# Differential-attention probabilities transposed by VectorE squares and a DRAM round trip, head index innermost, values later in TensorE's order

## The reference

```python
# differential attention: two 64-dim maps per head, value dim 128
sc = jnp.einsum('bqhcd,bkhcd->bhcqk', qb, kf) * scale      # c = 0, 1
p = jax.nn.softmax(jnp.where(causal, sc, -jnp.inf), axis=-1)
attn = p[:, :, 0] - lam * p[:, :, 1]
oa = rms_norm(jnp.einsum('bhqk,bkhe->bqhe', attn, vf), subln_w) * (1 - lambda_init)
# sparse attention: an indexer scores keys, the 64 best causal keys per query are kept
score = jnp.einsum('bqhk,bqh->bqk', jax.nn.relu(jnp.einsum('bqhd,bkd->bqhk', qi, ki)), wi)
_, idx = lax.top_k(jnp.where(causal, score, -jnp.inf), 64)
ob = softmax(q . k_sel) @ v_sel
mix = concatenate([oa * silu(dg), ob * silu(sg)]);  x = x + rms_norm(mix @ w_out, post_w)
```

## Time and profile before

| | |
|---|---|
| median of three runs | 303.1 us (302.99 to 303.43) |
| the profiled execution, its own time | 302.85 us |
| its span, first to last instruction | 301.1 us |
| TensorE busy | 292.4 us (97%) |
| TensorE weight loads busy | 246.4 us (82%) |
| VectorE busy | 234.9 us (78%) |
| ScalarE busy | 163.9 us (54%) |
| GpSimd busy | 67.6 us (22%) |
| DMA queue of SyncE, share of 16 engines | 62.8% |
| granted TensorE clock, mean | 0.996 of full speed |

### The profile page before, as it was taken

The page is one execution under the profiler, slowest core; times in us unless marked ns, Lnnn a source line. Parts: engine busy times, 40 slices in busy tenths (PEclk is TensorE's granted clock), DMA queues, the critical chain, the costliest instruction groups (busy, mean ns, idle before and its releaser), DMA issues.

```text
span 301.1 us, 4401 instructions
## 1 busy us (share of the span) xinstructions
PE 292.4 (97%) x1568; PEld 246.4 (82%) x1568; DVE 234.9 (78%) x474; ACT 163.9 (54%) x284; POOL 67.6 (22%) x116
## 2 busy tenths in 40 slices
PE   8999999999999999999999999999999999999992
PEld 7799777788787888788888988778878788887892
DVE  4752989899999997955984786878999999787343
ACT  5986963736577473603665855473737747390101
POOL 6558210303030220101060740012303030210101
PEclk9999999999999999999999999999999999999998
DMA  7999959457518569860059799937653675742011
GB/s 242 370 371 386 371 214 354 135 143 227 195 69 210 209 211 303 191 201 23 0 158 369 242 350 250 325 108 204 209 150 131 146 272 152 202 70 72 0 70 70
DMA packets 62229, 60.01 MB, mean 199 GB/s; under 512 B 34560, under 2 KB 39424, under 8 KB 62208
## 3 DMA queue, kind: packets, MB, share of 16 engines
q1 hardware_dynamic: 61920, 59.47, 62.8%
q10 hardware_dynamic: 288, 0.26, 0.3%
HBM read 54.48 MB, written 5.24 MB: 198 GB/s over the span
## 4 chain that ended last, share of the span: by engine, by line
PE 40%; DVE 37%; ACT 8%; DMA 6%; POOL 4%; issue 3%; SPq 1%; POOLq 0%; DVEq 0%; ACTq 0%
DVE w_lo L987 14%; PE bank_a L470 8%; PE bank_a L461 7%; PE bank_a L466 7%; PE bank_s L618 6%; DMA w_raw<-in_w_in 6%; PE bank_a L618 5%; ACT xt_pbuf L831 4%; DVE work L1107 4%; DVE xt_pbuf L1124 3%; DVE top L1106 3%; DVE xt_pbuf L1140 3%; DVE mixn L1150 2%; DVE mixn L1036 2%; PE bank_s L559 1%
## 5 line engine op out<-in xcount | busy, mean ns | idle before, releaser
L987 DVE TENSOR_TENSOR w_lo<-w_raw,w_hi 128x2048 fp32r<-128x2048 f32 (+1 forms) x46 | 98.8, 2154 | 18.5 <-ACT w_hi L763 18.3
L763 ACT ACTIVATE w_hi<-w_raw 128x2048 fp32r<-128x2048 f32 (+1 forms) x46 | 81.9, 1784 | 31.9 <-PE bank_a L470 23.4
L461 PE MATMUL bank_a<-w_hi,h_hi 128*128 128x512 f32 (+1 forms) x272 | 72.5, 388 | 0.0
L470 PE MATMUL bank_a<-w_lo,h_hi 128*128 128x512 f32 (+1 forms) x272 | 70.0, 379 | 0.5 <-DVE w_lo L987 0.5
L466 PE MATMUL bank_a<-w_hi,h_lo 128*128 128x512 f32 (+1 forms) x272 | 69.9, 379 | 0.0
L470 PEld LDWEIGHTS bank_a<-w_lo,h_hi 128*128 128x128 f32 x272 | 49.7, 188 | 10.5 <-DVE w_lo L987 1.0
L466 PEld LDWEIGHTS bank_a<-w_hi,h_lo 128*128 128x128 f32 x272 | 49.8, 188 | 9.8
L461 PEld LDWEIGHTS bank_a<-w_hi,h_hi 128*128 128x128 f32 x272 | 47.9, 188 | 10.4 <-issue 2.7
L831 ACT ACTIVATE xt_pbuf<-xt_pbuf,st 128x128 f32<-128x128 f32 (+1 forms) x48 | 21.3, 444 | 25.1 <-DVE st L1124 25.1
L1417 POOL TENSOR_TENSOR rt<-nat,tab 128x256 f32<-128x256 f32 x10 | 7.4, 741 | 112.5 <-ACT nat L815 112.5
L815 ACT ACTIVATE nat<-bank_a,st 128x512 f32<-128x512 f32 x20 | 13.5, 681 | 19.6 <-PE bank_a L470 19.6
(11 more groups left out here) (196 smaller groups left out, 431.1 us busy)
## 6 DMA issues: line engine op xcount, KB each, us to landing
w_raw<-in_w_in SPq DMA_DIRECT2D x30, 1024.0 KB, 6.0
w_raw<-in_w_out SPq DMA_DIRECT2D x8, 1024.0 KB, 6.1
w_raw<-in_w_in SPq DMA_DIRECT2D x8, 584.0 KB, 7.3
turned<-mixn SPq DMA_DIRECT2D x20, 128.0 KB, 2.7
prm<-in_rows SPq DMA_DIRECT2D x2, 705.0 KB, 7.0
w_raw<-in_w_in SPq DMA_DIRECT2D x2, 512.0 KB, 6.3
xres<-in_x SPq DMA_DIRECT2D x2, 512.0 KB, 9.5
dqT<-turned SPq DMA_DIRECT2D x2, 512.0 KB, 5.9
```

The source lines that it names most:

```text
L461: pe.matmul(bank, h_hi[:, HALF * half + kk, tok], whi[:, kk, :], start=half == 0 and kk == 0, stop=False)
L470: mm = pe.matmul(bank, h_hi[:, HALF * half + kk, tok], wlo[:, kk, :], start=False, stop=half == 1 and kk == HALF - 1)
L763: act.activation(unit(w_hi, u), unit(raw, u), ACT.Copy).then_inc(hi_done.sem, 1)
L987: dve.tensor_tensor(unit(w_lo, u), unit(raw, u), unit(w_hi, u).bitcast(F32), ALU.subtract).then_inc(lo_done.sem, 1)
```

## The change

1. The three TensorE turns of the differential probabilities go (12 transposes a layer), and with them their three drains on VectorE. In their place stand three `dve.transpose` of 128x512, four `put` DMAs for each and one `get` for each. The squares are staged in `mixn`, and in the two halves of `nat[:, 1]`.
2. In all DRAM-turned tensors (queries of all three mixers, PD and PS) the slot (head, or block and head) becomes the innermost index. VectorE writes its squares with a step of 8 floats (4 floats for PD and PS0), the DRAM runs grow to 256 floats (128 for PD and PS0), and TensorE's stationary tile is read with that step (`gathered`).
3. In TensorE's order `values(0)` moves from behind `dsa_scores(12)` to behind `first(18)`, and `values(1)` from ahead of `second(18)` to behind `turn_mix(T_MD0)`. They wait for the landing of the DMAs in place of the drains.
4. The squares of the sparse queries are staged in `iqT` and not in `mixn`; so the drain of T_SK, which writes over `iqT`, waits for their `put`.
5. On VectorE one round of `choose(1, ...)` comes behind the combine of PD1B's heads, and `gate_dsa(0)` comes ahead of the drain of T_MD1. The T banks are numbered anew (13 uses a layer in place of 16).

```diff
-T_IK, T_DK, T_PD0, T_PD1A, T_SK, T_PD1B = 4, 5, 7, 8, 9, 11
-T_MD0, T_MD1, T_MS0, T_MS1 = 12, 13, 14, 15
+T_IK, T_DK, T_SK = 4, 5, 7
+T_MD0, T_MD1, T_MS0, T_MS1 = 9, 10, 11, 12
+IQS, DQS, SQS, PD0, PD1A, PD1B, PS0, PS1 = range(8)
...
+        def gathered(buf, s, parts=slice(0, P), slots=BLOCKS * HEADS):
+            return buf[parts, :].rearrange("p (t s) -> p s t", s=slots)[:, s, :]
+        def by_column(buf):
+            return buf.rearrange("p (j c s) -> p s j c", j=SQUARES, c=LANES)
...  SyncE
-                    to = scratch[n].rearrange("(j r) a (i c) -> i r a j c", j=SQUARES, i=SQUARES)[i]
+                    to = scratch[n].rearrange("(j r) i m -> i r j m", j=SQUARES)[i]
...
                     if u == 16:
                         sp.wait_ge(sq_squares.sem, sq_squares.at(layer, 1))
-                        put(2, squares, sq_put.sem)
+                        put(SQS, iqT, sq_put.sem)
+                        put_probs(layer, PD0)
                     if u == 17:
                         sp.wait_ge(sq_put.sem, sq_put.at(layer, 16 * SQUARES))
-                        get(2, sqT, sq_landed.sem)
+                        get(SQS, sqT, sq_landed.sem)
+                        put_probs(layer, PD1A)
+                        get_probs(layer, PD0)
+                    if u == 18:
+                        put_probs(layer, PD1B)
+                        get_probs(layer, PD1A)
+                        get_probs(layer, PD1B)
...  TensorE
-                        mm = pe.matmul(bank[:, i * n:(i + 1) * n], sqT[:, b, h, :],
+                        mm = pe.matmul(bank[:, i * n:(i + 1) * n], gathered(sqT, b * HEADS + h),
...
-                pe.wait_ge(combined.sem, combined.at(layer, 1))
-                turn_probs(T_PD0, 6, 0, HEADS)
                 diff_scores(10, 1, (2, 3))
                 second(15)
-                pe.wait_ge(combined.sem, combined.at(layer, 2))
-                turn_probs(T_PD1A, 8, 1, 2)
...
-                pe.wait_ge(combined.sem, combined.at(layer, 3))
-                turn_probs(T_PD1B, 10, 1, 2)
                 pe.wait_ge(t_drained.sem, t_drained.at(layer, T_SK + 2))
                 pe.wait_ge(sq_landed.sem, sq_landed.at(layer, sq_landed.per_layer))
                 dsa_scores(12, 0, range(HEADS))
-                pe.wait_ge(t_drained.sem, t_drained.at(layer, T_PD0 + 1))
-                values(0, 0, v_diff, [[slot(0, h)] for h in range(HEADS)], place(layer, DV, 0) + 1)
                 second(17)
                 first(18)
+                pe.wait_ge(prob_landed[PD0].sem, prob_landed[PD0].at(layer, 16))
+                values(0, 0, v_diff, [[gathered(pT[:, 0, :], h, slots=HEADS)] for h in range(HEADS)], ...)
                 dsa_scores(13, 1, (0, 1))
                 dsa_scores(14, 1, (2, 3))
-                pe.wait_ge(t_drained.sem, t_drained.at(layer, T_PD1B + 1))
-                values(1, 1, v_diff, ...)
                 second(18)
                 turn_mix(T_MD0, 0, 0)
+                pe.wait_ge(prob_landed[PD1A].sem, prob_landed[PD1A].at(layer, 16))
+                pe.wait_ge(prob_landed[PD1B].sem, prob_landed[PD1B].at(layer, 16))
+                values(1, 1, v_diff, ...)
                 first(19)
...  VectorE
-                    dve.transpose(squares, nat[:, slot, :, :].rearrange("p b n -> p (b n)")).then_inc(done, 1)
+                    dve.transpose(by_column(iqT[:, :] if rope == 4 else squares), nat[:, slot, :, :].rearrange("p b (f j c) -> p (b f) j c", j=SQUARES, c=LANES)).then_inc(done, 1)
...
+                turn_squares(1, 4, sq_squares.sem)
                 dve.wait_ge(dq_put.sem, dq_put.at(layer, 16 * SQUARES))
-                turn_squares(1, 4, sq_squares.sem)
+                turn_probs(PD0, 6)
                 split_lo(layer, 16)
                 combine(8, 1, 2, 0)
-                drain(T_PD0, pT[:, 0, :])
+                dve.wait_ge(sq_squares.sem, sq_squares.at(layer, 1))
+                turn_probs(PD1A, 8)
                 mask_scores(10, 1, 2, causal[:, :])
                 mask_scores(11, 1, 2, causal[:, :])
                 split_lo(layer, 17)
+                choose(1, 1)
+                combine(10, 1, 2, 2)
+                turn_probs(PD1B, 10)
                 choose(1, 2)
-                drain(T_PD1A, pT[:, 1, :])
-                combine(10, 1, 2, 2)
-                choose(1, 1)
                 mask_unchosen(1)
+                dve.wait_ge(sq_put.sem, sq_put.at(layer, 16 * SQUARES))
                 drain_pair(T_SK, skT)
                 split_lo(layer, 18)
-                drain(T_PD1B, pT[:, 2, :])
                 mask_scores(12, 0, 4, work[0][:, :])
...
+                gate_dsa(0)
                 drain_mix(T_MD1, m_hi, m_lo, 1, subln)
-                gate_dsa(0)
```

More of the change, by code:

```diff
@@ L86 @@
 ROW_N = sum(ROW.values())
-T_IK, T_DK, T_PD0, T_PD1A, T_SK, T_PD1B = 4, 5, 7, 8, 9, 11
-T_MD0, T_MD1, T_MS0, T_MS1 = 12, 13, 14, 15
-T_USES = 16
-PS0, PS1 = range(3, 5)
+T_IK, T_DK, T_SK = 4, 5, 7
+T_MD0, T_MD1, T_MS0, T_MS1 = 9, 10, 11, 12
+T_USES = 13
+IQS, DQS, SQS, PD0, PD1A, PD1B, PS0, PS1 = range(8)
+SLOT = {PD0: 0, PD1A: 1, PD1B: 2, PS0: 0}
 LANES = 32
@@ L175, in build_trunk @@
         squares = mixn[:, :, :].rearrange("p b n -> p (b n)")
-        prob_buf = {PS0: dkT[:, 0:2, :].rearrange("p f t -> p (f t)"), PS1: dqT[:, :, :, :].rearrange("p b f t -> p (b f t)")}
+        prob_buf = {PD0: mixn[:, 0, :], PD1A: nat[:, 1, 0, :], PD1B: nat[:, 1, 1, :], PS0: dkT[:, 0:2, :].rearrange("p f t -> p (f t)"), PS1: dqT[:, :]}
         A = [pb("bank_a0", [P, WIDTH]), pb("bank_a1", [P, WIDTH])]
@@ L240, in build_trunk @@
         rq_ready = count("rq_ready", BLOCKS)
-        prob_squares = count("prob_squares", 2)
-        prob_put = {n: count(f"prob_put{n}", 16 * SQUARES) for n in range(PS0, PS1 + 1)}
-        prob_landed = {n: count(f"prob_landed{n}", 16) for n in range(PS0, PS1 + 1)}
+        prob_squares = count("prob_squares", 5)
+        prob_put = {n: count(f"prob_put{n}", 16 * SQUARES) for n in range(PD0, PS1 + 1)}
+        prob_landed = {n: count(f"prob_landed{n}", 16) for n in range(PD0, PS1 + 1)}
         subln_ready = count("subln_ready", 1)
@@ L257, in build_trunk @@
         pool_setup = sem("pool_setup")
-        ends = (S[1], T[0])
+        ends = (S[1], T[1])
         last_ms = st[:, 153:154]
@@ L317, in put @@
                 for i in range(SQUARES):
[L318 to L319 removed]
+                    to = scratch[n].rearrange("(j r) i m -> i r j m", j=SQUARES)[i]
+                    sp.dma_start(to, buf[i * LANES:(i + 1) * LANES, :].rearrange("r (j m) -> r j m", j=SQUARES)).then_inc(written, 16)
             def put_probs(layer, n):
[L322 removed]
+                sp.wait_ge(prob_squares.sem, prob_squares.at(layer, n - PD0 + 1))
                 put(n, prob_buf[n], prob_put[n].sem)
@@ L640, in body @@
                     for n in range(2):
-                        for i in range(4):
-                            f, b = 2 * n + i // 2, i % 2
-                            mm = pe.transpose(S[n][:, i * P:(i + 1) * P], nat[:, 0, b, f * P:(f + 1) * P], ident[:, :])
+                        for f in range(HEADS):
+                            mm = pe.transpose(S[n][:, f * P:(f + 1) * P], nat[:, 0, n, f * P:(f + 1) * P], ident[:, :])
                         mm.then_inc(iq_filled, 1)
@@ L714, in body @@
                 pe.wait_ge(prob_landed[PS0].sem, prob_landed[PS0].at(layer, 16))
-                values(2, 0, v_dsa, [[slot(0, h)] for h in range(HEADS)], place(layer, SV, 0) + 1)
+                values(2, 0, v_dsa, [[gathered(pT[:, 0, :], h, slots=HEADS)] for h in range(HEADS)], place(layer, SV, 0) + 1)
                 pe.wait_ge(t_drained.sem, t_drained.at(layer, T_MD0 + 1))
@@ L727, in body @@
                 pe.wait_ge(prob_landed[PS1].sem, prob_landed[PS1].at(layer, 16))
-                values(3, 1, v_dsa, [[slot(1 + h // 2, 2 * (h % 2) + t) for t in range(2)] for h in range(HEADS)],
+                values(3, 1, v_dsa, [[gathered(pT[:, 1:3, :].rearrange("p s n -> p (s n)"), 2 * h + t) for t in range(2)] for h in range(HEADS)],
                        place(layer, SV, 1) + 1)
@@ L1035, in turn_squares @@
                     dve.wait_ge(rope_done.sem, rope_done.at(layer, rope))
-                    dve.transpose(squares, nat[:, slot, :, :].rearrange("p b n -> p (b n)")).then_inc(done, 1)
+                    dve.transpose(by_column(iqT[:, :] if rope == 4 else squares), nat[:, slot, :, :].rearrange("p b (f j c) -> p (b f) j c", j=SQUARES, c=LANES)).then_inc(done, 1)
                 def turn_probs(n, use):
-                    dve.wait_ge(exps_done.sem, exps_done.at(layer, use + 1 - S_DIFF0))
-                    probs = pbuf[:, 0, :] if n == PS0 else pbuf[:, 1:3, :].rearrange("p s n -> p (s n)")
-                    dve.transpose(prob_buf[n], probs).then_inc(prob_squares.sem, 1)
+                    if n >= PS0:
+                        dve.wait_ge(exps_done.sem, exps_done.at(layer, use + 1 - S_DIFF0))
+                    else:
```

(5 more changed lines are left out.)

47 lines of the change are left out of this document (22 added, 25 removed).

## The result

The changed kernel takes 327.58 us, median of 4 runs (326.33 to 327.91); the kernel before takes 303.05 us beside it (302.99 to 303.43). The ratio is 1.080, 95% interval 1.077 to 1.083: 24.5 us slower. The forecast was 304.0 with a range of 302 to 316. Slower was right; the size was not (0.9 us forecast, 24.5 measured), and the likeliest case was the wrong one.

What follows compares the result with a forecast made beforehand. TensorE and VectorE were taken to bound the kernel together with hardly any slack. T_MS0 came 1.0 us later less the 0.54 stall, 0.44 a layer, 0.9 in two: 303.75 on the profiled run, 304.0 as median, range 302.0 to 316.

Steps and rivals of the forecast that it cites:

- the likeliest case: The forecast itself: 304.0 us for the whole kernel, own range 303.0 to 305, chance 0.42.
- The two unknown prices: VectorE writing and TensorE loading with a step of 16 or 32 bytes; both taken as costing nothing extra.
- the low end: VectorE's squares priced as contiguous: 1.17 us for 1024 columns, 0.63 for 512; for TensorE's loads, 0.
- the high end: VectorE's squares at twice the low end; TensorE's loads doubled from 103 ns, 56 records, 5.7 us a layer.
- Rival 1: Strided squares cost double on VectorE: 4.2 us ahead of handover (a) pass to T_MS0, PS1's 1.17 between gates; chance 0.33.
- The row behind the high end: Profile row taken as a VectorE stream at half its rate: 560 against 292 ns for 128 columns.
- handover (a): VectorE's drains of T_SK to TensorE, slack about 0.35 us; sparse scores forecast about 0.5 us later, TensorE's 1.4 us gone.
- The gate chain: ScalarE, GpSimd, VectorE from values(0) to gate 0: gate 1.0 us later, no stall at T_MD0, T_MD1 1.0 us later.
- The gain behind it: gate_dsa(0) no longer waits for T_MD1's drain; the 0.54 us stall at T_MS0 goes, leaving 0.44 us later a layer.
- The parts taken at nothing: DMA work: PD1B in pT by 110 for use at 117, PD0 by 101 for use at 111; no cost.
- Rival 3: TensorE's saved time comes through: 0.3 to 1.4 us less a layer, 300.5 to 302.4 us; chance 0.15.

Runs made afterwards that it cites:

- e2: e1 but TensorE loads its stationary tiles with the step of 8 or 4 floats, operands wrongly ordered; 321.25 us, ratio 1.061.
- e4: The kernel before in its own order, with the head innermost in everything that goes through DRAM, PD still turned by TensorE; 315.45 us, ratio 1.041.
- e3: e1 but VectorE writes its squares and layer 0's index queries with the step, TensorE loads contiguous tiles; 312.90 us, ratio 1.032.
- e8: e1 with a step of 2 floats in VectorE's squares and TensorE's loaded tiles, operands wrongly ordered; 306.61 us, ratio 1.0115.
- e1: The changed kernel without any step: squares written side by side, contiguous tiles loaded, operands wrongly ordered; 305.32 us, ratio 1.008.
- e6: e5 with combine(10) behind two rounds of choose on VectorE, so behind GpSimd's rotation; 304.72 us, ratio 1.0059.
- e7: The kernel before with gate_dsa(0) ahead of the drain of T_MD1 on VectorE; 301.11 us, ratio 0.9941.
- e5: Complete kernel: the changed kernel's order and DRAM round trips, with the layout of before (head outermost, runs of 128 bytes); 305.35 us, ratio 1.0076.
- e9: e6 with values(0) and values(1) back in their old places, still from the DRAM round trip; 304.19 us, ratio 1.0042.
- e10: e9 with T_SK's turn behind first(17) and second(17) ahead of dsa_scores(12); 303.1 to 309.3 us, without the three longest median 304.5, ratio 1.0064.

## Why the prediction was wrong, step by step

**The step that failed** is "The two unknown prices": "I take the low end, the same instruction" for VectorE's squares and "I take 0" for TensorE's loads. Neither was free. A 1024-column square steps 2.00 us (91.04 to 93.04) where 1.17 was taken and 2.34 was the high end, and a 512-column one 0.95 (93.04 to 93.99) where 0.63 was taken and 1.26 the high end: 0.7 and 0.5 of the way up. A record of the values steps 217 ns where 103 was taken; the addition, 114 ns, is above the high end of one doubling. In the whole: 15.9 us by the loads (e2), 7.6 by the squares and the clock that fell with them (e3).

**The loads' count was short as well.** The high end had 56 records from scores 12 on; there are 64 (16 of the sparse scores, 48 of the values), of which the 8 with 256 moving columns pay only 0.11 us in all. Those of the index scores and the differential scores, 64 a layer, also read with the step and add 1.4 us twice in each layer. That they lie ahead of the handovers did not hide those in e4, where the sum of all of them is what was measured. Counted in full the loads alone add 2 x 9.8 to 304, which is 323.6, and the range ended at 316.

**Rival 1**, in its variant with the loads (317), had the right mechanism and 10.6 us too little: it put the loads at a fifth of their high end. The squares it put too high, 5.4 us a layer for 3.8 in e3. The rule of the Trainium skill ("SBUF — State Buffer", Door 1, its note on cachelines: 16-byte lines, two hits a line for full bandwidth) agrees with these runs on both engines, e8 above all: two floats apart nearly free, four and eight apart 1.6 to 1.8 times the time for a square or a load. By the rule that any stride goes in the plain mode ("VectorE: DVE Perf Modes" of the Trainium skill, Mode 1x) it works but is not as fast: 1233 ns contiguous, 2175 with the step.

**The row behind the high end was misread.** The 560 ns of the earlier trace rows, taken for a VectorE stream at half its rate, is two operations that each ran beside GpSimd's rotation of another operand (in layer 0 at 69.91, with GpSimd busy from 68.52 to 71.15). In the changed kernel the same instruction comes behind that rotation (73.25, the rotation ends at 73.13) and takes 295 ns:

```profile
L1118 DVE TENSOR_TENSOR work<-work,causal 128x128 f32<-128x128 f32 x2 | 0.6, 295 | 0.1
```

It says nothing of steps, and that the high end it gave was of the right order is luck. What it does show is the contention that handover (a) left out.

**Handover (a)** was right in kind: VectorE's list puts T_SK's drains later and TensorE's 1.4 us are lost there (1.04 us of stall in e1). Its size was not: the sparse scores of e1 start 1.3 us later than before, and not 0.5. The missing term is on VectorE: its operations of `combine(10)` beside GpSimd's rotation, 0.8 us, of which e6 gets back half by moving them.

**The gate chain** was right: idle 2.15 us ahead of gate 0 in e1 released by GpSimd (2 or more forecast), the short first operation of 0.20 us, T_MD1 stalls (0.33), T_MS0 does not, no wait at T_MD0. Shifted by the 0.8 us, gate 0 was forecast at 114.65 and came at 115.58, 0.9 later.

**The gain behind it** was right: e7 earns it alone, and 0.7 us a layer where 0.54 was taken.

**The parts taken at nothing**, the DMA work, were at nothing in this order (e1 against e5); with the values in their old places a landing is waited for (0.33 us in e9).

**Rival 3**, TensorE's time coming through, did not occur in any of the kernels with the round trip (e5, e6, e9, e10).

## What to carry to other kernels

That the count of elements stays the same does not make an innermost step free: price it by a row of the same engine with such a step, or take the dear end, above all where a layout chosen for DMA is read by TensorE with few moving columns. Before a slow row serves as a price, look in the timeline at what ran beside it. When work is taken from an engine that is dense, list every handover that it reaches next, those over a third engine too, before counting the time as earned; the cheap gain here was an exchange of two items in VectorE's list, 1.8 us by the runs and 1.4 by the trace, and not the 2.8 us of TensorE work.

## What the runs showed of the hardware

- 128-column fp32 weight loads take 187 to 192 ns contiguous, 192 to 196 with a step of 8 bytes, 327 to 335 with 16 or 32. With 256 moving columns the load is nearly covered (1.84 against 1.73 us for eight); with 128 it is not (1.74 against 0.82).
- VectorE's square transpose of 1024 columns: 1233 to 1240 ns contiguous, 1241 at 8 bytes, 2175 at 32; 512 columns 702 to 712 contiguous, 714 at 8 bytes and 1103 at 16.
- A stall of TensorE of 1.90 us was followed by a granted clock of 0.64 over 8 us (e3); the changed kernel, with stalls of 0.51, 1.29 and 1.36 us in the same stretch of layer 0, kept 1.00 there. In e10 0.60 and 0.72 followed a stall of 3.01 us, and 1.00 one of 1.43.
- Some operations of VectorE slow beside GpSimd: the two of `combine(10)` take 1.43 us beside the rotation and 0.88 behind it (e1, e6), a 128x128 operation 562 ns beside one and 295 behind it (e1, changed kernel). The two of MAX8 and MATCH_REPLACE8 beside the rotation in e6 keep their 0.43 and 0.41 us.
- GpSimd slows beside VectorE as well: its first operation of 128x4 takes 1.71 us (before) and 1.39 (e9) beside a split of VectorE and ends within 0.1 us of it, and 0.20 with VectorE idle (e1).
